# A gated feed-forward stage started on unnormed input: the norm's factor moved from the stage's input to its gate tiles and to the output tiles of the down product

## The chip, the core and the metric

The kernel runs on one core of a Trainium2 chip, in one launch. TensorE (PE) multiplies matrices into PSUM banks; VectorE (DVE) and ScalarE (ACT) work element by element on SBUF and PSUM; SyncE (SP) issues the loads. Each engine works through its own instructions in order and waits on semaphores for the others. The metric is the device time of an execution in microseconds (us), lower is better.

## The reference, cut to what matters

The kernel computes two blocks of a transformer, one after the other, for a sequence of 256 positions (and 256 of context in the first block) and a width of 1024. The change touches the two gated feed-forward layers of the second block:

```python
def rms_norm_2(x, g):
    xf = x.astype(jnp.float32)
    y = xf * lax.rsqrt(jnp.mean(xf * xf, axis=-1, keepdims=True) + EPS)
    return (y * g.astype(jnp.float32)).astype(x.dtype)
...
    val, gate = jnp.split(xn @ w_up, 2, axis=-1)
    gp = jnp.pad(gate, ((0, 0), (CONV_W - 1, 0), (0, 0)))
    gc = conv_b + conv_w[0] * gp[:, 0:seq]
    for j in range(1, CONV_W):
        gc = gc + conv_w[j] * gp[:, j:j + seq]
    return (jax.nn.silu(gc) * val) @ w_down
...
            h = h + s5_mixer(rms_norm_2(h, a_norm[i]), ...)
...
            h = h + sb_mixer(rms_norm_2(h, b_norm[j]), b_w_q[j], b_q_norm[j], k, v, b_w_o[j])
        h = h + conv_ffn(rms_norm_2(h, ffn_norm[layer]), ffn_w_up[layer], ffn_conv_w[layer],
                         ffn_conv_b[layer], ffn_w_down[layer])
```

Layer 0 takes the s5 mixer, which ends in a gated product (the stage glu), layer 1 the sb mixer, which ends in a product (the stage wo2); w_up has 2 x 2816 columns. The factor of the norm, 1/sqrt(mean(h^2) + eps), is one number for each position. It commutes with the product by w_up. The value's factor also commutes with the product by w_down; the gate's does not, since the convolution mixes positions and silu isn't linear.

## The kernel before

All activations are stored transposed: 128 partitions of the width by the positions, so that a tile of a product is 128 x 256. h is the residual stream, eight such tiles (KT = 8). Every product is made in three: each operand is split into a high part and a rest (u_hi, u_lo; w_hi, w_lo), and `products` (L697 to L699) adds hi x hi, lo x hi and hi x lo in a PSUM bank.

**Weights.** They come as units of 128 x 1024 through a ring of four slots. SyncE loads a unit into raw (512 KB), ScalarE copies it to w_hi (L1127), VectorE takes the rest as w_lo (L1548). At step n of a stage both engines split unit n + 3 of it; ScalarE may do so once TensorE has finished tile n - 1, whose slot it is.

**Stages.** The program is a list of stages (`make_plan`). Every engine walks the same list with its own part. A stage of one-unit tiles takes 24 products for a tile, and its output tiles go round the four banks of TILE. The stages around the change are: glu (16 tiles; two make one tile of h: value x sigmoid(gate) is added to h), fup0 (44 tiles, value and gate of 22 pairs), fdown0 (8 tiles of 22 x 3 products, added to h), k2, ...; and wo2 (8 tiles, added to h), fup1, fdown1, with which the kernel ends.

**The norm.** In glu and in wo2 ScalarE squares each new tile of h (L1198, L1172) and VectorE adds the squares up in ssum (L1684); after the stage TensorE sums over the partitions with two small products (`row_total`, L786: one for ssum, one for the last square). Then ScalarE takes logarithm and exponential of the mean (L1382, L1384), VectorE refines with a Newton step (L1830, L1815 to L1817) into rsn, and for each of eight tiles VectorE makes h x gain x rsn (L1846), ScalarE its high part u_hi (L1391) and VectorE the rest u_lo (L1859). TensorE starts fup on these with three tiles side by side, so that it can use each operand tile as it comes (`first_tiles`, KT_FIRST).

**A gated pair.** When the gate tile is done, ScalarE makes f_c = bank x conv_w[2] + conv_b (L1207), VectorE adds the two shifted terms (L1693, L1695) and multiplies by the value bank to f_h (L1698: this frees the pair's two banks, semaphore d1); ScalarE takes the sigmoid (L1211), VectorE multiplies it in (L1704), ScalarE copies to f_hi (L1216), VectorE makes f_lo (L1709). TensorE waits for d1 of pair q - 2 before it starts tile 2q.

**Late norms.** Three stages start without their norm already: win, k2 and q2. The stage ahead of them has a `prep`: after each new tile of h ScalarE makes u_hi = h x gain (`next_hi`, L1223) and VectorE u_lo (`next_lo`, L1639) from unnormed h. TensorE puts `row_total` into its first tile, after the sixth of eight products, and `late_norm` on VectorE and ScalarE, queued behind the first w_lo and w_hi of the stage, makes the factor, which is put on the output tiles.

Of the kernel before, what the change touches and what calls it, by code (L numbers as in the profile page):

```python
# [13 lines left out]
P = 128  # L14
# [45 lines left out]
def increments(s):  # L60
# [15 lines left out]
    elif s.kind == "MLP":  # L76
        c.update(a1=n, d1=n)
    elif s.kind == "UP":
        c.update(a1=n // 2, conv=n // 2, d1=n // 2, a2=n // 2, d2=n // 2, a3=n // 2, f_lo=n // 2)
    elif s.kind == "GLU":  # L80
        c.update(d1=n // 2, d2=n // 2, a2=n // 2, a3=n // 2, d3=n // 2 - 1, sq=1)
# [9 lines left out]
def make_plan():  # L91
# [18 lines left out]
        Stage("glu", "GLU", 16),  # L110
        Stage("fup0", "UP", 2 * FT),
# [4 lines left out]
        Stage("wo2", "RES", 8, norm=True),  # L116
        Stage("fup1", "UP", 2 * FT),
# [37 lines left out]
def program(nc, weights, ada_w, ada_b, x_t, vecs, cons, bias_na, ssm_in, ssm_bc, scratch, out):  # L155
# [5 lines left out]
    with ctx:  # L161
# [76 lines left out]
        f_h = place("f_h", [P, 2, SEQ], at=fx + 4096)  # L238

# [69 lines left out]
        def sem(name):  # L309
# [23 lines left out]
            "dv": sem("dve_mean"), "uh": sem("next_hi"), "ul": sem("next_lo"),  # L333
# [121 lines left out]
        NORM_COLS = {n: slice(SEQ, TOK) for n in ("q2",)}  # L455
# [3 lines left out]
        PREPARED = {"win": ("down1b", 1, 0), "k2": ("fdown0", 2, 0), "q2": ("fdown0", 2, 1)}  # L459

        LATE_NORM = {"a": 4, "kv": 6}

        ROOTS = {"mix0": 0, "mlp0": 1, "mix1": 2, "mlp1": 3, "ffn0": 5, "ffn1": 7}
# [3 lines left out]
        NORM_BEFORE = {"qk0": 0, "up0a": 1, "q1": 2, "up1a": 3, "fup0": 4, "fup1": 5}  # L467
# [106 lines left out]
        def _(pe):  # L574
# [71 lines left out]
            KT_FIRST = ("qk0", "up0a", "q1", "up1a", "glu", "fup0", "fup1")  # L646
# [403 lines left out]
            row_total("glu")  # L1050
            drained("glu")
# [54 lines left out]
            gemm("wo2"); row_total("wo2"); drained("wo2")  # L1106
# [4 lines left out]
        def _(act):  # L1111
# [22 lines left out]
            def tile(s, i, jj, body, first=False):  # L1134
# [101 lines left out]
            def late_norm(name):  # L1236
# [1214 lines left out]
```

## Time and profile before

| | |
|---|---|
| median of 3 runs | 1763.11 us (1760.55 to 1763.88) |
| the profiled execution's own time | 1763.66 us |
| its span, first to last instruction | 1761.9 us |
| TensorE (PE) busy | 1631.2 us, 93% |
| weight loads (PEld) busy | 1439.2 us, 82% |
| VectorE (DVE) busy | 1300.2 us, 74% |
| ScalarE (ACT) busy | 867.7 us, 49% |
| mean granted TensorE clock | 0.964 of 2.4 GHz |
| moved by DMA | 290.74 MB, mean 165 GB/s |

The busy times are averages over stages with different limits. The profile also lists, for each instruction, its start, its duration and, in brackets, how long its engine had been idle before it and which instruction of which line released it. The start-to-start distance of two instructions of one engine can be less than the duration, since they overlap a little.

### The profile page before, as it was taken

Reading aid. Unit: us, or ns where it says so; the run is one execution under the profiler, and the core shown is the slowest. Engines: PE = TensorE matmul, PEld = TensorE weight load, DVE = VectorE, ACT = ScalarE, POOL = GpSimd, SP = SyncE. Lnnn points to the kernel's source line nnn. Section 1 sums busy time; section 2 is a strip of 40 time slices with the busy share of each in tenths; the row PEclk is TensorE's granted clock in tenths of the full one; section 3 lists DMA queues with packets and bytes.
Section 4 is the critical chain, followed back from the end, with each engine's and each line's share of the span. In section 5 each row is a group of like instructions: output and inputs, shape, how many; then the busy total and the mean of one; then the engine's idle time right before and its main releaser. Section 6 shows DMA issues by size and latency. Waiting matters only on the chain.

```text
span 1761.9 us, 32639 instructions
## 1 busy us (share of the span) xinstructions
PE 1631.2 (93%) x11892; PEld 1439.2 (82%) x11892; DVE 1300.2 (74%) x2195; ACT 867.7 (49%) x1497; POOL 96.5 (5%) x152
## 2 busy tenths in 40 slices
PE   5899999899999999689899999698999998889999
PEld 3677866688888888575799999598999988589999
DVE  4899797788768867778678786866876676468764
ACT  4555386343223434547564554255555576445553
POOL 0001030000000024000001111100000000000000
PEclk9899999999999999898999999799999999999999
DMA  9236651435667855330356668444656544036564
GB/s 358 84 108 230 211 147 44 134 127 185 203 194 242 265 163 170 98 96 1 93 178 216 211 198 337 167 132 132 190 182 191 189 141 134 13 120 194 180 198 143
DMA packets 79626, 290.74 MB, mean 165 GB/s; under 512 B 10000, under 2 KB 11792, under 8 KB 77600
## 3 DMA queue, kind: packets, MB, share of 16 engines
q1 hardware_dynamic: 69120, 249.03, 43.2%
q0 software_dynamic: 10400, 40.30, 6.9%
q8 instruction: 67, 1.10, 0.3%
q14 instruction: 39, 0.32, 0.1%
HBM read 270.61 MB, written 18.68 MB: 164 GB/s over the span
## 4 chain that ended last, share of the span: by engine, by line
PE 76%; DVE 13%; ACT 5%; issue 3%; DMA 2%; DVEq 0%; ACTq 0%; SPq 0%; POOLq 0%
PE bank L697 22%; PE bank L698 21%; PE bank L699 21%; DVE stat L2043 2%; PE bank L762 1%; PE bank L764 1%; PE bank L763 1%; DMA raw<-weights 1%; DVE prob L2062 1%; PE bank L907 1%; ACT w_hi L1127 1%; PE bank L918 1%; DVE w_lo L1548 1%; PE bank L775 1%; PE bank L931 1%
## 5 line engine op out<-in xcount | busy, mean ns | idle before, releaser
L697 PE MATMUL bank<-u_hi,w_hi 128*128 128x256 f32 (+1 forms) x1936 | 618.1, 319 | 42.5 <-DVE u_lo L1861 25.6
L698 PE MATMUL bank<-u_lo,w_hi 128*128 128x256 f32 (+1 forms) x1936 | 606.7, 313 | 0.0
L699 PE MATMUL bank<-u_hi,w_lo 128*128 128x256 f32 (+1 forms) x1936 | 606.2, 313 | 0.0
L1548 DVE TENSOR_TENSOR w_lo<-raw,w_hi 128x1024 fp32r<-128x1024 f32 x372 | 452.3, 1222 | 189.9 <-ACT w_hi L1127 176.3
L1127 ACT ACTIVATE w_hi<-raw 128x1024 fp32r<-128x1024 f32 x360 | 376.3, 1050 | 185.0 <-PE bank L699 154.9
L697 PEld LDWEIGHTS bank<-u_hi,w_hi 128*128 128x128 f32 x1936 | 378.7, 196 | 69.8 <-issue 46.9
L698 PEld LDWEIGHTS bank<-u_lo,w_hi 128*128 128x128 f32 x1936 | 378.5, 196 | 22.0 <-issue 3.0
L699 PEld LDWEIGHTS bank<-u_hi,w_lo 128*128 128x128 f32 x1936 | 378.2, 195 | 18.9
L697 PE MATMUL bank<-hid_hi,w_hi 128*128 128x512 f32 (+1 forms) x512 | 174.0, 340 | 0.0
L699 PE MATMUL bank<-hid_hi,w_lo 128*128 128x512 f32 (+1 forms) x512 | 172.1, 336 | 0.0
L698 PE MATMUL bank<-hid_lo,w_hi 128*128 128x512 f32 (+1 forms) x512 | 172.1, 336 | 0.0
L697 PEld LDWEIGHTS bank<-hid_hi,w_hi 128*128 128x128 f32 x512 | 97.2, 190 | 11.0 <-issue 1.5
L699 PEld LDWEIGHTS bank<-hid_hi,w_lo 128*128 128x128 f32 x512 | 97.1, 190 | 10.1
L698 PEld LDWEIGHTS bank<-hid_lo,w_hi 128*128 128x128 f32 x512 | 97.2, 190 | 9.7
L1561 DVE SCALAR_TENSOR_TENSOR ada_raw<-ada_raw,silu_row 128x1024 f32<-128x1024 f32 x80 | 97.4, 1221 | 6.4 <-DMA ada_raw<-ada_w 6.1
L698 PE MATMUL bank<-f_lo,w_hi 128*128 128x256 f32 x352 | 99.6, 283 | 0.0
L697 PE MATMUL bank<-f_hi,w_hi 128*128 128x256 f32 x352 | 99.6, 283 | 0.0
L699 PE MATMUL bank<-f_hi,w_lo 128*128 128x256 f32 x352 | 99.6, 283 | 0.0
L1180 ACT ACTIVATE rs<-bank 128x512 f32<-128x512 f32 (+1 forms) x64 | 31.4, 491 | 125.9 <-PE bank L699 119.4
L1172 ACT ACTIVATE sq<-h 128x256 f32 (+3 forms) x48 | 23.3, 484 | 97.5 <-DVE h L1601 83.4
L698 PEld LDWEIGHTS bank<-f_lo,w_hi 128*128 128x128 f32 x352 | 67.6, 192 | 0.0
L697 PEld LDWEIGHTS bank<-f_hi,w_hi 128*128 128x128 f32 x352 | 67.6, 192 | 0.0
(320 smaller groups left out, 2299.5 us busy)
## 6 DMA issues: line engine op xcount, KB each, us to landing
raw<-weights SPq DMA_DIRECT2D x372, 512.0 KB, 3.5
ada_raw<-ada_w SPq DMA_DIRECT2D x80, 512.0 KB, 4.1
ada_first<-ada_w SPq DMA_DIRECT2D x16, 512.0 KB, 15.5
bias_sb<-bias_na POOLq DMA_DIRECT2D x16, 256.0 KB, 3.3
toep_dram<-zeros POOLq DMA_DIRECT2D x8, 512.0 KB, 9.0
bat_dram<-bat POOLq DMA_DIRECT2D x16, 256.0 KB, 4.1
ca_dram<-ca POOLq DMA_DIRECT2D x16, 256.0 KB, 3.9
s_bat<-bat_dram POOLq DMA_DIRECT2D x4, 1024.0 KB, 7.7
```

What stands on the lines that cost most here:

```text
L697: pe.matmul(dst, wh, hi[:, kt, xs], start=first, stop=False)
L698: pe.matmul(dst, wh, lo[:, kt, xs], start=False, stop=False)
L699: return pe.matmul(dst, wl, hi[:, kt, xs], start=False, stop=final)
L762: pe.matmul(dst, hi[:, kt, xs], wh, start=first and tt % 2 == 0, stop=False, skip_group_check=True)
L763: pe.matmul(dst, lo[:, kt, xs], wh, start=False, stop=False, skip_group_check=True)
L764: mm = pe.matmul(dst, hi[:, kt, xs], wl, start=False, stop=final, skip_group_check=True)
L1127: A(w_hi[:, slot, :], raw[:, slot, :], ACT.Copy).then_inc(S["hi"], 1)
L1172: A(sq[:, jj % 2, 0:s.tok], h[:, bass.ds(j, 1), 0:s.tok].rearrange("p a t -> p (a t)"), ACT.Square).then_inc(S["a1"], 1)
L1180: chain.link(A(rs[:, b2, 0:s.tok], bank[:, 0:s.tok], ACT.Relu))
L1548: TT(w_lo[:, slot, :], raw[:, slot, :], w_hi[:, slot, :].bitcast(F32), ALU.subtract).then_inc(S["lo"], 1)
L1561: STT(raw_, raw_, 1.0, silu_row[:, 0, :], ALU.mult, ALU.mult, accum_out=ada_acc[:, b, a % 4, 0:1]).then_inc(S["ada_read"], 1)
L2043: red = dve.tensor_reduce(stat[:, 0, b, :], both[:, :, 0:keys], AX.X, ALU.max, negate=True)
```

## The change

The stages glu and wo2 get a `prep`, and fup0 and fup1 become late stages: they multiply unnormed u from the columns 256 to 511 of u_hi and u_lo. The root sits behind the first w_hi and w_lo of fup. A new VectorE instruction in each pair (`gate_scaled`, L1701 after) multiplies the gate bank by rsn into an SBUF tile f_g, from which ScalarE and the two shifted terms of the convolution read. The value stays unnormed through f_h, f_hi, f_lo and the down product, and in fdown0 and fdown1 VectorE multiplies each output tile by rsn before it is added to h. The work on a pair is also spread otherwise over the steps: convolution and sigmoid of a pair now come in the two steps after its gate tile.

```diff
@@ -107,14 +107,14 @@
         Stage("win", "IN", 8, late="a"),
-        Stage("glu", "GLU", 16),
-        Stage("fup0", "UP", 2 * FT),
+        Stage("glu", "GLU", 16, prep=(("ffn0", SEQ),)),
+        Stage("fup0", "UP", 2 * FT, late="ffn0"),
...
         Stage("v2", "V", 8),
-        Stage("wo2", "RES", 8, norm=True),
-        Stage("fup1", "UP", 2 * FT),
+        Stage("wo2", "RES", 8, norm=True, prep=(("ffn1", SEQ),)),
+        Stage("fup1", "UP", 2 * FT, late="ffn1"),
@@ -452,19 +453,20 @@
-        NORM_COLS = {n: slice(SEQ, TOK) for n in ("q2",)}
+        NORM_COLS = {n: slice(SEQ, TOK) for n in ("q2", "fup0", "fup1")}
...
-        PREPARED = {"win": ("down1b", 1, 0), "k2": ("fdown0", 2, 0), "q2": ("fdown0", 2, 1)}
-
-        LATE_NORM = {"a": 4, "kv": 6}
-
-        ROOTS = {"mix0": 0, "mlp0": 1, "mix1": 2, "mlp1": 3, "ffn0": 5, "ffn1": 7}
+        PREPARED = {"win": ("down1b", 1, 0), "k2": ("fdown0", 2, 0), "q2": ("fdown0", 2, 1),
+                    "fup0": ("glu", 1, 0), "fup1": ("wo2", 1, 0)}
+
+        LATE_NORM = {"a": 4, "ffn0": 5, "kv": 6, "ffn1": 7}
+
+        ROOTS = {"mix0": 0, "mlp0": 1, "mix1": 2, "mlp1": 3}
...
-        NORM_BEFORE = {"qk0": 0, "up0a": 1, "q1": 2, "up1a": 3, "fup0": 4, "fup1": 5}
+        NORM_BEFORE = {"qk0": 0, "up0a": 1, "q1": 2, "up1a": 3}
@@ -643,7 +645,7 @@
-            KT_FIRST = ("qk0", "up0a", "q1", "up1a", "glu", "fup0", "fup1")
+            KT_FIRST = ("qk0", "up0a", "q1", "up1a", "glu")
@@ -1047,8 +1049,6 @@
-            row_total("glu")
-            drained("glu")
@@ -1103,7 +1103,7 @@
             pe.wait_ge(sb_l, 8)
-            gemm("wo2"); row_total("wo2"); drained("wo2")
+            gemm("wo2")
@@ -1182,11 +1182,13 @@
                     pair = i * 2 + jj // 2
+                    if first and jj < 2:
+                        return
                     if jj % 2 == 0:
-                        if not first or jj:
-                            hidden(s, pair - 1, 1 - jj // 2)
+                        gate_input(s, pair - 1, 1 - jj // 2)
                     else:
-                        gate_silu(s, pair, jj // 2, n_done, bank)
+                        gate_sigmoid(s, pair - 1, 1 - jj // 2)
+                        hidden(s, pair - 1, 1 - jj // 2)
@@ -1197,15 +1199,18 @@
-
-            def gate_silu(s, pair, pb, n_done, bank):
+                    next_hi(s, pair, 0)
+
+            def gate_input(s, pair, pb):
                 layer = int(s.name[-1])
-                act.wait_ge(S["unit"], n_done)
+                act.wait_ge(S["g1"], value("g1", s, pair + 1))
                 act.wait_ge(S["d1"], value("d1", s, pair - 1))
-                A(f_c[:, pb, :], bank[:, 0:SEQ], ACT.Identity, bias=VC("conv_b", layer * FT + pair),
+                A(f_c[:, pb, :], f_g[:, pb, :], ACT.Identity, bias=VC("conv_b", layer * FT + pair),
...
+
+            def gate_sigmoid(s, pair, pb):
@@ -1241,6 +1246,8 @@
                     root(rsn[:, 0:SEQ], ssum[:, 0:SEQ]).then_inc(n_rs, 1)
+                    if name in ("ffn0", "ffn1"):
+                        act.preload_act_table_set("sigmoid_and_others")
@@ -1287,7 +1294,8 @@
                         one(i + 1)
-                    hidden(s, s.tiles // 2 - 1, 1)
+                    for step in (gate_input, gate_sigmoid, hidden):
+                        step(s, s.tiles // 2 - 1, 1)
@@ -1497,8 +1505,7 @@
             stage("glu")
-            norm(4, "ffn0")
-            act.preload_act_table_set("sigmoid_and_others")
+            act.preload_act_table_set("natural_log_exp_and_others")
@@ -1594,7 +1600,11 @@
                     if gate is None:
-                        TT(dcol(h, j, all_), bank[:, all_], dcol(h, j, all_), ALU.add).then_inc(S["d1"], 1)
+                        part = bank
+                        if s.name in HIDDEN:
+                            part = tmp[:, b2, :]
+                            link(TT(part[:, all_], bank[:, all_], rsn[:, all_], ALU.mult))
+                        TT(dcol(h, j, all_), part[:, all_], dcol(h, j, all_), ALU.add).then_inc(S["d1"], 1)
@@ -1613,12 +1623,12 @@
                 elif s.kind == "UP":
+                    if first and jj < 2:
+                        return
                     if jj % 2 == 0:
-                        if not first or jj:
-                            hidden_lo(s, i * 2 + jj // 2 - 1, 1 - jj // 2)
+                        gate_conv(s, i * 2 + jj // 2 - 1, 1 - jj // 2)
                     else:
-                        gate_conv(s, i, jj // 2, jj)
-                        gated(s, i * 2 + jj // 2, jj // 2)
+                        gated(s, i * 2 + jj // 2 - 1, 1 - jj // 2)
@@ -1628,6 +1638,7 @@
                         add_row(s, "a3", pair, pb)
+                    next_lo(s, pair, 0)
@@ -1683,10 +1694,16 @@
-            def gate_conv(s, i, pb, jj):
-
-                layer, pair = int(s.name[-1]), i * 2 + pb
-                val, gate = TILE[(s.tile0 + jj - 1) % RING], TILE[(s.tile0 + jj) % RING]
+            def gate_scaled(s, pair, pb):
+
+                dve.wait_ge(S["unit"], pair * 2 + (CREDIT + s.unit0 + 2))
+                dve.wait_ge(S["conv"], value("conv", s, pair - 1))
+                TT(f_g[:, pb, :], TILE[(s.tile0 + 2 * pb + 1) % RING][:, 0:SEQ], rsn[:, 0:SEQ], ALU.mult).then_inc(S["g1"], 1)
+
+            def gate_conv(s, pair, pb):
+
+                layer = int(s.name[-1])
+                val, gate = TILE[(s.tile0 + 2 * pb) % RING], f_g[:, pb, :]
@@ -1749,6 +1766,10 @@
                             n = jj * s.units + k
+                            if s.kind == "UP" and jj % 2 == 0 and not (first and jj == 0):
+                                gate_scaled(s, i * 2 + jj // 2 - 1, 1 - jj // 2)
+                                if not first:
+                                    hidden_lo(s, i * 2 + jj // 2 - 2, jj // 2)
@@ -1794,7 +1815,12 @@
                         one(i + 1)
-                    hidden_lo(s, s.tiles // 2 - 1, 1)
+                    last_pair = s.tiles // 2 - 1
+                    gate_scaled(s, last_pair, 1)
+                    hidden_lo(s, last_pair - 1, 0)
+                    gate_conv(s, last_pair, 1)
+                    gated(s, last_pair, 1)
+                    hidden_lo(s, last_pair, 1)
```

Not shown are the semaphore g1 of the new tile, its place in SBUF, and the calls `norm(4, "ffn0")` and `norm(5, "ffn1")` that go from VectorE's and ScalarE's programs.

Where fup0 starts, VectorE's rows were, from the last tiles of the norm on, up to the first pair:

```order
L1846 SCALAR_TENSOR_TENSOR tmp<-h,vec,rsn 128x256
L1859 TENSOR_TENSOR u_lo<-tmp,u_hi 128x256 x2
L1548 TENSOR_TENSOR w_lo<-raw,w_hi 128x1024 x2
L1693 SCALAR_TENSOR_TENSOR f_c<-bank,vec,f_c 128x255
L1695 SCALAR_TENSOR_TENSOR f_c<-bank,vec,f_c 128x254
L1698 TENSOR_TENSOR f_h<-f_c,bank 128x256
L1704 TENSOR_TENSOR f_h<-f_h,f_sig 128x256
```

and are, from the last tile of glu on:

```order
L1650 SCALAR_TENSOR_TENSOR u_lo<-h,vec,u_hi 128x256
L1554 TENSOR_TENSOR w_lo<-raw,w_hi 128x1024
L1680 TENSOR_SCALAR ssum<-bank 128x256
L1841 TENSOR_TENSOR ssum<-ssum,rsn 128x256
L1842 TENSOR_TENSOR ssum<-ssum,rsn 128x256
L1843 SCALAR_TENSOR_TENSOR rsn<-ssum,rsn 128x256
L1554 TENSOR_TENSOR w_lo<-raw,w_hi 128x1024
L1701 TENSOR_TENSOR f_g<-bank,rsn 128x256
L1554 TENSOR_TENSOR w_lo<-raw,w_hi 128x1024
L1710 SCALAR_TENSOR_TENSOR f_c<-f_g,vec,f_c 128x255
L1712 SCALAR_TENSOR_TENSOR f_c<-f_g,vec,f_c 128x254
L1715 TENSOR_TENSOR f_h<-f_c,bank 128x256
```

Now the root stands behind one w_lo of the stage, and the first f_h behind three, as against two.

In the loop over four tiles, VectorE's rows of one pair of tiles were, with the rows for registers and waits:

```order
L1548 TENSOR_TENSOR w_lo<-raw,w_hi 128x1024
L1708 REGISTER_ALU
L1709 ISA
L1709 TENSOR_TENSOR f_lo<-f_h,f_hi 128x256
L1547 REGISTER_ALU
L1548 TENSOR_TENSOR w_lo<-raw,w_hi 128x1024
L1692 REGISTER_ALU
L1693 ISA
L1693 SCALAR_TENSOR_TENSOR f_c<-bank,vec,f_c 128x255
```

and are, at the same place:

```order
L1701 TENSOR_TENSOR f_g<-bank,rsn 128x256
L1725 REGISTER_ALU
L1726 ISA
L1726 TENSOR_TENSOR f_lo<-f_h,f_hi 128x256
L1553 REGISTER_ALU
L1554 TENSOR_TENSOR w_lo<-raw,w_hi 128x1024
L1709 REGISTER_ALU
L1710 ISA
L1710 SCALAR_TENSOR_TENSOR f_c<-f_g,vec,f_c 128x255
```

The gate product stands ahead of f_lo and of the w_lo in front of the convolution; the other w_lo moved from before f_lo to between f_h and its product with the sigmoid.

TensorE's rows at the end of glu, from the end of that stage's loop on, were:

```order
L400 COMPARE_AND_BRANCH
L786 MATMUL bank<-ssum,con 128x256
L786 MATMUL bank<-sq,con 128x256
L697 MATMUL bank<-u_hi,w_hi 128x256
L698 MATMUL bank<-u_lo,w_hi 128x256
L699 MATMUL bank<-u_hi,w_lo 128x256
```

and are, in the first tile of fup0, after 18 of its 24 products:

```order
L700 MATMUL bank<-u_lo,w_hi 128x256
L701 MATMUL bank<-u_hi,w_lo 128x256
L788 MATMUL bank<-ssum,con 128x256
L788 MATMUL bank<-sq,con 128x256
L699 MATMUL bank<-u_hi,w_hi 128x256
L700 MATMUL bank<-u_lo,w_hi 128x256
```

The row sum moved from between the stages into the next stage's first tile.

## Rows read from the trace of the kernel before

**Rows 1.** The page, part 4: the chain of waits by engine.
```profile
PE 76%; DVE 13%; ACT 5%; issue 3%; DMA 2%; DVEq 0%; ACTq 0%; SPq 0%; POOLq 0%
```

**Rows 2.** Timeline of TensorE at the stages' bounds: start, us, engine, line, what.
```profile
1199.27 0.60 PE L786 MATMUL bank<-ssum,con 128*128 128x256 f32 x2
...
1335.47 0.28 PE L697 MATMUL bank<-f_hi,w_hi 128*128 128x256 f32 x1
...
1559.25 0.28 PE L699 MATMUL bank<-u_hi,w_lo 128*128 128x256 f32 x1
...
1695.57 0.28 PE L697 MATMUL bank<-f_hi,w_hi 128*128 128x256 f32 x1
```

**Rows 3.** Stretches: us, then PE, PEld, DVE, ACT, POOL busy, PEclk, DMA share, GB/s.
```profile
1199.27:1206.85 7.58, 1.30 (x7) 0.53 (x5) 4.00 (x10) 3.78 (x7) 0.00 (x0) 0.74 0.38 133
1206.85:1209.75 2.90, 2.90 (x13) 2.90 (x14) 2.59 (x7) 1.25 (x3) 0.00 (x0) 0.50 0.03 6
1209.75:1335.50 125.75, 125.42 (x1045) 125.23 (x1045) 98.66 (x156) 72.15 (x111) 0.00 (x0) 1.00 0.57 175
...
1416.00:1418.00 2.00, 2.00 (x19) 2.00 (x18) 1.73 (x5) 1.42 (x4) 0.00 (x0) 1.00 0.32 74
1433.00:1435.00 2.00, 2.00 (x11) 2.00 (x11) 1.83 (x5) 1.41 (x4) 0.00 (x0) 0.50 0.69 246
```

**Rows 4.** Timeline at the start of win: row sum on TensorE, factor on VectorE.
```profile
1079.23 0.60 PE L786 MATMUL bank<-ssum,con 128*128 128x256 f32 x2
...
1080.21 0.28 PE L698 MATMUL bank<-u_lo,w_hi 128*128 128x256 f32 x1
...
1081.06 0.42 DVE L1669 TENSOR_SCALAR ssum<-bank 128x256 f32<-128x256 f32 x1
...
1082.88 0.43 DVE L1816 TENSOR_TENSOR ssum<-ssum,rsn 128x256 f32<-128x256 f32 x1
1083.34 0.42 DVE L1817 SCALAR_TENSOR_TENSOR rsn<-ssum,rsn 128x256 f32<-128x256 f32 x1
```

**Rows 5.** Timeline of ScalarE at the ends of glu and of fdown0.
```profile
1201.06 0.42 ACT L1198 ACTIVATE sq<-h 128x256 f32 x1 [1.13 <-DVE h L1628]
...
1399.77 0.51 ACT L1223 ACTIVATE u_hi<-h,vec  x1 [1.83 <-DVE h L1597]
```

**Rows 6.** Timeline of VectorE and ScalarE in fup1 and at its end.
```profile
1587.64 1.22 DVE L1548 TENSOR_TENSOR w_lo<-raw,w_hi 128x1024 fp32r<-128x1024 f32 x1
1588.78 0.47 DVE L1693 SCALAR_TENSOR_TENSOR f_c<-bank,vec,f_c 128x255 f32<-128x255 f32 x1
1589.40 0.48 DVE L1695 SCALAR_TENSOR_TENSOR f_c<-bank,vec,f_c 128x254 f32<-128x254 f32 x1 [0.15 <-DVE f_c L1693]
1589.92 0.42 DVE L1698 TENSOR_TENSOR f_h<-f_c,bank 128x256 f32<-128x256 f32 x1
...
1698.38 0.42 DVE L1704 TENSOR_TENSOR f_h<-f_h,f_sig 128x256 f32<-128x256 f32 x1
1698.84 0.42 ACT L1216 ACTIVATE f_hi<-f_h 128x256 fp32r<-128x256 f32 x1 [0.58 <-DVE f_h L1704]
1699.16 1.04 ACT L1127 ACTIVATE w_hi<-raw 128x1024 fp32r<-128x1024 f32 x1
1700.23 1.23 DVE L1548 TENSOR_TENSOR w_lo<-raw,w_hi 128x1024 fp32r<-128x1024 f32 x1 [0.52 <-ACT w_hi L1127]
```

**Rows 7.** Timeline of ScalarE: the table load ahead of fup1 and what follows.
```profile
1571.03 1.28 ACT L1529 ACT_TABLE_LOAD   x1
1572.32 1.06 ACT L1127 ACTIVATE w_hi<-raw 128x1024 fp32r<-128x1024 f32 x1
```

**Rows 8.** Timeline of VectorE in wo2: tile 6 is added to h.
```profile
1558.08 0.42 DVE L1597 TENSOR_TENSOR h<-bank,h 128x256 f32<-128x256 f32 x1
```

**Rows 9.** Timeline of TensorE in k2 and q2: two waits, for a square.
```profile
1415.22 0.70 PE L775 MATMUL bank<-sq,con 128*128 128x256 f32 x2 [1.67 <-ACT sq L1145]
...
1430.78 0.48 PE L775 MATMUL bank<-sq,con 128*128 128x256 f32 x1 [2.07 <-ACT sq L1145]
```

More of the change, by code:

```diff
@@ L78, in increments @@
     elif s.kind == "UP":
-        c.update(a1=n // 2, conv=n // 2, d1=n // 2, a2=n // 2, d2=n // 2, a3=n // 2, f_lo=n // 2)
+        c.update(g1=n // 2, a1=n // 2, conv=n // 2, d1=n // 2, a2=n // 2, d2=n // 2, a3=n // 2, f_lo=n // 2)
     elif s.kind == "GLU":
@@ L238, in program @@
         f_h = place("f_h", [P, 2, SEQ], at=fx + 4096)
+        f_g = place("f_g", [P, 2, SEQ], at=fx + 6144)
         pw = place("pw", [P, 3, 2, POW, PAIRS], at=big + 32768)
@@ L332, in program @@
             "f_lo": sem("dve_hidden_lo"),
-            "dv": sem("dve_mean"), "uh": sem("next_hi"), "ul": sem("next_lo"),
+            "g1": sem("dve_gate"), "dv": sem("dve_mean"), "uh": sem("next_hi"), "ul": sem("next_lo"),
         }
@@ L1527, in _ @@
                     A(u_hi[:, p, 0:SEQ], psum[6 + p % 2][:, 0:SEQ], ACT.Copy).then_inc(sb_h, 1)
-            stage("wo2"); norm(5, "ffn1")
-            act.preload_act_table_set("sigmoid_and_others")
+            stage("wo2")
             stage("fup1"); stage("fdown1")
@@ L1534, in _ @@
         def _(dve):
-            for n in ("lo", "mod", "d1", "d2", "d3", "conv", "f_lo", "dv", "ul"):
+            for n in ("lo", "mod", "d1", "d2", "d3", "conv", "f_lo", "dv", "ul", "g1"):
                 dve.nop().then_inc(S[n], CREDIT)
@@ L2174, in _ @@
                     step(m)
-            stage("glu"); norm(4, "ffn0")
+            stage("glu")
             stage("fup0"); stage("fdown0")
@@ L2198, in _ @@
                     TT(u_lo[:, p, 0:SEQ], psum[6 + p % 2][:, 0:SEQ], u_hi[:, p, 0:SEQ].bitcast(F32), ALU.subtract).then_inc(sb_l, 1)
-            stage("wo2"); norm(5, "ffn1")
+            stage("wo2")
             stage("fup1"); stage("fdown1")
```

## The prediction

> **What bounds the kernel now.** The chain of waits comes first: 76% of the span is TensorE [rows 1]. So what counts is where TensorE does not multiply at full pace. The timeline of TensorE gives the two stages that the change touches. fup0: the sum of squares of glu is begun at 1199.27 and the first product of fdown0 starts at 1335.47; fup1: wo2's last product starts at 1559.25, so TensorE is free at 1559.37, and fdown1's first product starts at 1695.57 [rows 2]. Both spans are 136.2 us. Each stage is 44 tiles of 24 products, 1056 products. The stretches show their pace: 1045 records in 125.75 us, with 0.33 us idle, is 0.12 us from start to start, at granted clock 1.00, and VectorE is busy for 98.66 us of it, 78% [rows 3]. 1056 x 0.12 = 126.7 us. So about 9.5 us of each stage is no product at full pace: a stretch of 7.58 us in which TensorE is busy 1.30 us (the root, Newton's step and the first normed tile), and then a stretch of 2.90 us with 13 products at granted clock 0.50, that is 1.2 GHz, after the idle time; at 0.12 they take 1.6 us [rows 3]. ScalarE and VectorE are slack behind TensorE in the rest of the stage.
>
> **What is removed.** The whole norm between the stages (9.5 us in each), and with it the idle time that put the clock down. fup0 now multiplies unnormed u, made tile by tile in glu and wo2. What takes its place is seen in the kernel already: the stage win starts this way. There the two halves of the row sum start at 1079.23, in the middle of the tile, and the second product after them starts at 1080.21 [rows 4]; without the sums it would start 0.12 after 1079.23. So the sums cost 0.86 us and nothing else waits.
>
> **Start of fup0.** Is the last operand ready? ScalarE's square at 1201.06 stays [rows 5]; the new u_hi follows 0.32 later (the step from f_hi to w_hi, 1698.84 to 1699.16 [rows 6]), takes 0.51 [rows 5] and ends at 1201.9; VectorE's u_lo ends at about 1202.4. TensorE has six column tiles of work (18 x 0.12 = 2.2 us, to 1201.4), then the sums up to 1202.3 and tile 6, so it needs the last u_lo at about 1202.6: hidden, with 0.2 us to spare. The factor is late next. ScalarE goes on with a table load (1.28 [rows 7]) to 1203.2, w_hi, and VectorE's w_lo 1.07 later (1699.16 to 1700.23 [rows 6]) at 1204.3. The norm's first step is queued behind this w_lo, 1.14 later (1587.64 to 1588.78 [rows 6]): 1205.4. From there the factor takes 2.70 us (1081.06 to 1083.34, plus 0.42 [rows 4]): 1208.1. Meanwhile ScalarE loads the sigmoid table, again 1.28, and starts the next w_hi at 1208.05; w_lo 1209.1, gate times factor 1210.3 (a 128x256 product of a PSUM bank and an SBUF tile, as f_h at 1589.92: 0.42 [rows 6]), w_lo 1210.7, the two convolution steps 1211.85 and 1212.5, f_h 1213.0 to 1213.4, with the spacings 1.14, 0.62, 0.52 of [rows 6]. Tile 4 of the stage needs the banks which that f_h frees; TensorE is there at 1199.27 + 0.86 + 4 x 2.88 = 1211.65. It waits **1.8 us**. Saved in fup0: 136.2 - 126.7 - 0.86 - 1.8 = **6.8 us**.
>
> **Start of fup1.** wo2 now makes u_hi and u_lo too. Its tiles hang in a ring of both engines (h, square, w_hi, w_lo, next h); u_hi adds 0.41 to each turn, which TensorE's pace absorbs only at tile 3. By tile 4 h is some 0.7 late, by tile 6 1.5: h at 1558.08 [rows 8] becomes 1559.6. The first tile of fup1 waits for that h (its own bank needs less): 1560.1, 0.7 after 1559.37. The square of tile 7 then holds up the second half of the sum by 0.1. No table needs loading before the root here. With the same spacings w_lo of unit 3 starts at 1564.0, the factor is ready at 1567.9, gate times factor at 1570.0, and f_h ends at 1573.2; TensorE asks for it at 1560.1 + 0.96 + 11.5 = 1572.55 and waits 0.65. Saved: 136.2 - 126.7 - 0.86 - 0.7 - 0.1 - 0.65 = **7.1 us**.
>
> **The loop.** Each pair of tiles gets one more VectorE instruction of 0.42: 78% busy becomes about 86%, below TensorE's 48 x 0.12 = 5.76 us per pair. But f_h, which frees the banks, now comes a tile later after its gate tile, and ScalarE's w_hi is queued behind f_hi. That closes a ring: gated product to f_hi 0.46, to w_hi 0.32, to w_lo 1.07, to the convolution 1.14, 0.62, f_h 0.52, to w_lo 0.34 (0.42 less the overlap of 0.08 that a 1.22 w_lo followed after 1.14 shows), to the next gated product 1.14 [rows 6]: **5.6 us**. Gate times factor and f_lo (0.45 + 0.34) lie in the 1.85 us between the gated product and its w_lo, in which VectorE has nothing else. So the ring keeps up, by only 0.15 us a pair, and costs nothing; cover gone, each 0.1 us over 5.76 costs 0.1 in each of some 40 pairs, 4 us. At the stage's end the last pair is finished about 5.8 us after TensorE leaves it; fdown needs it 7.6 us in, after 21 x 0.36. The convolution reading the SBUF copy instead of the bank I take at no change; the other SBUF forms of this size stand at 0.42.
>
> **Down tiles.** 16 products by the factor, 0.46 each (1082.88 to 1083.34, linked [rows 4]), hide under 7.9 us per tile except the last of each stage. After fdown0, ScalarE and VectorE go straight from the last h through u_hi at 1399.77 [rows 5] into the table load and the k2 stage, in which TensorE waits for their squares [rows 9]; 0.46 late stays 0.46. After fdown1 the last h ends the kernel: 0.46. Bounds for the pair: 0 to 0.92; I take 0.92.
>
> **The sum.** 6.8 + 7.1 - 0.9 = 13.0 us off the profiled execution's own 1763.66 (span 1761.9): 1750.7. That execution lies 0.55 above the median of the runs, 1763.11, so the forecast for the median is **1750.1**.
>
> **Clock and tables, the two uncertain prices.** After 1.67 us idle at 1415.22 the clock stays at 1.00; after 2.07 us at 1430.78 a stretch reads 0.50 [rows 3, 9]. About 16 products at that level cost 16 x 0.09 = 1.5 us. My wait at tile 4 of fup0 lies between the two, nearer the first, so I charge nothing; k2's wait grows from 1.67 to 2.13 and may fall too, mostly hidden, since that stage is bound by the other engines.
> On tables the trace shows 1571.03 plus 1.28 and the next ScalarE instruction at 1572.32 [rows 7]: 1.3 us for a switch. The Trainium skill, page "ScalarE: Activation LUTs", section "What ACT_TABLE_LOAD costs", adds a drain of about 1.38 us to each switch, 2.66 us in all. It would speak against this change, which puts two switches in front of the factor in fup0 and one in fup1; the sum would lose some 4 us by it, and by the row nothing. No row of this trace shows the drain.
>
> **Rivals.**
> 1. The forecast's case, ring under 5.76: chance 0.62, 1747 to 1754.
> 2. More waits at the starts (a fallen clock at tile 4 and in k2, 1.5 each; a switch of tables dearer than its row by as much again, 3 x 1.3): 8 to 10 us saved, 1753 to 1755. Against it: rows at 1.3 and 1.67. Chance 0.15.
> 3. The ring is a little over TensorE's pace, 5.85 to 6.0: 40 x 0.1 to 0.25 us of waits, 4 to 10 us lost, 1754 to 1760. For it: the margin is 0.15 us over eight summed spacings, some taken outside the loop. Chance 0.13.
> 4. **Slower.** VectorE does the gate product and f_lo on the ring, not beside it (if ScalarE's w_hi comes early, or f_hi late): 5.6 + 0.45 + 0.34 = 6.4, 0.65 x 40 = 26 us of waits against 13 saved: 1776. It decides from a ring of 6.1 us on. Against it: the gap of 1.85 us. Chance 0.05.
> 5. The change doesn't do what it says: TensorE still waits for the factor at the stage's start. The order of its instructions, sums inside the first tile, leaves little room: 0.05, about 1763.
>
> **How the numbers follow.** A measurement of this kernel tells about 0.2%, 3.5 us. Faster: cases 1, 2, and most of 3, 0.89. Same: rest of 3 and case 5, 0.06. Slower: 0.05. The low end is case 1 with the two waits at tile 4 and the 0.9 us not there: 1763.1 - 16.3 = 1746.8. The high end takes in case 2 and the lower part of 3: 1756.5.
>
> **What the profile after would show.** Row sum records about 2 us after the stages' starts with products on both sides; no 0.50 in PEclk there; a wait of TensorE for f_h at tile 4, about 1.8 and 0.65 us; one for h at fup1's start, 0.7; f_h of a pair every 5.76 us; stages of 129.4 and 129.1 us instead of 136.2. I am wrong if TensorE waits for f_h at every pair, if f_h records lie over 5.8 us apart, or if the clock falls inside the stages.

## The result, and the profile after it

The changed kernel takes 1752.3 us, the median of 6 runs (1750.73 to 1753.12); the kernel before, run again beside it, takes 1764.37 us (1760.55 to 1768.17, 6 runs). The ratio is 0.9937, with a 95% interval of 0.9927 to 0.9947: faster, by 0.63%. The profiled execution took 1750.73 us, its span is 1748.9 us, 13.0 less than the span of before. Its mean granted clock is 0.968. VectorE is now busy for 1312.5 us (75%), TensorE for 1627.1 us (93%).

The page's part 4, the chain by engine, reads as in [rows 1] but for a point here and there; TensorE still sets the time:

```profile
PE 75%; DVE 14%; ACT 6%; issue 4%; DMA 2%; ACTq 0%; DVEq 0%; SPq 0%; POOLq 0%
```

The timeline of TensorE shows the two stages; [rows 2] are its counterpart:

```profile
1200.33 0.60 PE L788 MATMUL bank<-ssum,con 128*128 128x256 f32 x2
...
1201.31 0.28 PE L700 MATMUL bank<-u_lo,w_hi 128*128 128x256 f32 x1
...
1212.45 0.36 PE L699 MATMUL bank<-u_hi,w_hi 128*128 128x256 f32 x1 [1.75 <-DVE f_h L1715]
...
1327.78 0.35 PE L699 MATMUL bank<-f_hi,w_hi 128*128 128x256 f32 x1
...
1552.20 0.28 PE L701 MATMUL bank<-u_hi,w_lo 128*128 128x256 f32 x1
1553.52 0.39 PE L699 MATMUL bank<-u_hi,w_hi 128*128 128x256 f32 x1 [1.04 <-DVE h L1607]
...
1555.78 0.60 PE L788 MATMUL bank<-ssum,con 128*128 128x256 f32 x2
1556.32 0.70 PE L788 MATMUL bank<-sq,con 128*128 128x256 f32 x2
...
1566.77 0.36 PE L699 MATMUL bank<-u_hi,w_hi 128*128 128x256 f32 x1 [0.41 <-DVE f_h L1715]
...
1682.13 0.36 PE L699 MATMUL bank<-f_hi,w_hi 128*128 128x256 f32 x1
```

The row sum at 1200.33 has 18 products of the stage's first tile ahead of it and the rest behind it. Those 18 take 18 x 0.12 = 2.16 us, so fup0 begins at 1198.17 and lasts until 1327.78: **129.6 us** instead of 136.2. fup1 lasts from wo2's end, 1552.32 (the last product's start plus 0.12), to 1682.13: **129.8 us** instead of 136.2. Three waits remain: for f_h at tile 4 of fup0 (1.75 us), for wo2's h at the start of fup1 (1.04), for f_h at tile 4 of fup1 (0.41). Behind the wait at tile 4 of fup0, and behind the row sum of fup1, the stretches up to the down product have the full clock, the first no idle time at all and the second only the 0.41 us; the columns are those of [rows 3]:

```profile
1212.45:1327.78 115.33, 115.33 (x961) 115.24 (x961) 95.22 (x161) 66.70 (x100) 0.00 (x0) 1.00 0.56 183
1556.32:1682.13 125.81, 125.40 (x1041) 125.11 (x1041) 103.53 (x174) 73.32 (x109) 0.00 (x0) 1.00 0.56 181
```

The slow stretch of [rows 3] at fup0's start, and the one at fup1's start (experiment 6), have no counterpart.

That the two stages shortened by 6.6 and 6.4 us, 13.0 together, and the whole span by 13.0 too, is partly chance. The factor on the down tiles takes 0.9 us back (experiment 8), and the profiled execution reached fup0 1.1 us sooner than that of before, at 1198.17 against 1199.27. That last point is not of the change: the profiled executions of the changed kernel and of all its variants below reach fup0 between 1197.98 and 1201.46.

What the prediction called the ring, a closed path in which VectorE waits for ScalarE and ScalarE for VectorE once in each pair of tiles, is in the timeline of the two engines in fup0. One turn, from one f_h (L1715) to the next:

```profile
1217.37 0.42 DVE L1715 TENSOR_TENSOR f_h<-f_c,bank 128x256 f32<-128x256 f32 x1
1217.71 1.22 DVE L1554 TENSOR_TENSOR w_lo<-raw,w_hi 128x1024 fp32r<-128x1024 f32 x1
1218.85 0.42 DVE L1721 TENSOR_TENSOR f_h<-f_h,f_sig 128x256 f32<-128x256 f32 x1
1219.18 0.42 DVE L1701 TENSOR_TENSOR f_g<-bank,rsn 128x256 f32<-128x256 f32 x1
1219.41 0.42 ACT L1221 ACTIVATE f_hi<-f_h 128x256 f32 x1 [1.62 <-DVE f_h L1721]
1219.73 1.04 ACT L1127 ACTIVATE w_hi<-raw 128x1024 fp32r<-128x1024 f32 x1
1219.99 0.43 DVE L1726 TENSOR_TENSOR f_lo<-f_h,f_hi 128x256 f32 x1 [0.39 <-ACT f_hi L1221]
...
1220.81 1.22 DVE L1554 TENSOR_TENSOR w_lo<-raw,w_hi 128x1024 fp32r<-128x1024 f32 x1 [0.39 <-ACT w_hi L1127]
...
1221.95 0.48 DVE L1710 SCALAR_TENSOR_TENSOR f_c<-f_g,vec,f_c 128x255 f32<-128x255 f32 x1
1222.57 0.48 DVE L1712 SCALAR_TENSOR_TENSOR f_c<-f_g,vec,f_c 128x254 f32<-128x254 f32 x1
1223.09 0.42 DVE L1715 TENSOR_TENSOR f_h<-f_c,bank 128x256 f32<-128x256 f32 x1
...
1228.92 0.42 DVE L1715 TENSOR_TENSOR f_h<-f_c,bank 128x256 f32<-128x256 f32 x1
```

The turns are 5.72 and 5.83 us, and so they alternate through both stages, 5.77 in the mean, against TensorE's 5.76 a pair: the margin is used up, but the excess is so small that the profile shows no idle time of TensorE behind tile 4. The new product of gate tile and factor (f_g, 0.42) and f_lo lie, as foreseen, between the gated product and w_lo, where VectorE is even idle twice.

### The profile page after: what moved, and what is told of

Its sections match the earlier page's. It is cut to its first block, busy times and chain, and to the rows that moved or that the text cites. A ratio compares the mean times of both kernels' runs of the same rounds, so it can differ in the third digit from the quotient of the medians.

```text
span 1748.9 us, 32745 instructions
## 1 busy us (share of the span) xinstructions
PE 1627.1 (93%) x11892; PEld 1435.7 (82%) x11892; DVE 1312.5 (75%) x2239; ACT 870.6 (50%) x1497; POOL 96.5 (6%) x152
## 4 chain that ended last, share of the span: by engine, by line
PE 75%; DVE 14%; ACT 6%; issue 4%; DMA 2%; ACTq 0%; DVEq 0%; SPq 0%; POOLq 0%
PE bank L699 21%; PE bank L701 21%; PE bank L700 21%; DVE stat L2069 2%; PE bank L764 1%; PE bank L766 1%; PE bank L765 1%; ACT w_hi L1127 1%; DVE w_lo L1554 1%; DVE prob L2088 1%; DMA raw<-weights 1%; PE bank L909 1%; PE bank L920 1%; PE bank L777 1%; PE bank L933 1%
## 5 line engine op out<-in xcount | busy, mean ns | idle before, releaser
L701 PEld LDWEIGHTS bank<-f_hi,w_lo 128*128 128x128 f32 x352 | 67.6, 192 | 0.0
```

Of the source, the lines that this page charges most:

```text
L701: return pe.matmul(dst, wl, hi[:, kt, xs], start=False, stop=final)
```

## Experiments

Two theories stood against each other at first. **The ring**: the loop's limit is one closed path through ScalarE and VectorE, and only work on this path costs time. **Load**: VectorE as a whole is near its limit (busy for 41.70 of 50 us here, 39.03 before), and any more work costs time. A third question was how much of the gain is the clock and how much the norm's own time. The ratios are to the kernel before, run on the same chip between the kernels: 1763.95 us (1760.82 to 1765.5) for 1, 2, 3 and the first of 7, 1762.83 (1761.05 to 1767.98) for 4, 5, 6 and 9, 1764.31 (1761.31 to 1765.13) for 8 and the second of 7.

**1. The changed kernel again**, as the level for the others.

> The changed kernel again, unaltered, as the level for the other runs of this chip. Theory (the norm and its slow stretch are gone, the loop is at the edge): 11 to 13 us below the kernel before, ratio 0.9925 to 0.994; TensorE waits 1.7 us at tile 4 of fup0, 1.0 at the start of fup1, 0.4 at its tile 4, and nothing else in the two stages. Rival (the 13 us of the one profiled execution were luck, and in other executions TensorE waits at pairs in the loop): some waits for f_h beyond the first, and 3 us or more between the stages' lengths here and 129.6 and 129.8 us.

Measured: 1750.98 us (1748.79 to 1753.89), ratio 0.9929 [0.9916, 0.9943], with the same waits (1.71, 1.03, 0.40).

**2 and 3. One more VectorE instruction of 0.42 us in each pair, on the ring and off it.** The instruction is the same in both, a product of the factor with itself into a tile that nobody reads:

```diff
 on the ring: gate_conv
                 TT(f_h[:, pb, :], c, val[:, 0:SEQ], ALU.mult).then_inc(S["d1"], 1)
+                TT(f_x[:, :], rsn[:, 0:SEQ], rsn[:, 0:SEQ], ALU.mult)
 off the ring: gate_scaled
                 ... rsn[:, 0:SEQ], ALU.mult).then_inc(S["g1"], 1)
+                TT(f_x[:, :], rsn[:, 0:SEQ], rsn[:, 0:SEQ], ALU.mult)
```

> One more VectorE product of 128x256 per pair (rsn by rsn into a scratch tile that nobody reads), put between f_h and the w_lo behind it. Ring theory: this place is on the ring, whose turn grows from 5.77 by 0.34 to 0.45 to about 6.1 to 6.2 us, TensorE waits for f_h at every pair, 0.35 to 0.45 x 40 pairs = 14 to 18 us more than the changed kernel: about 1767, at or above the kernel before. Rival (what counts is VectorE's load: 4.5 us before, 4.97 after, 5.4 here of 5.76 us): it still fits, no change, 1752.

> The same extra VectorE product, but put between gate times factor and f_lo, where VectorE stands idle 0.39 us until f_hi is there. Ring theory: off the ring, costs 0 to 1 us over both stages, 1752 to 1753, f_h still every 5.77 us. Rival (VectorE's load counts, wherever it stands): the same cost as between f_h and w_lo, both nothing or both 14 us and more.

Measured: on the ring **1764.5 us** (1763.59 to 1766.99), ratio 1.0009 [1.0, 1.0018]: 13.5 us over run 1, the whole gain is gone. Off the ring **1750.74 us** (1749.0 to 1753.49), ratio 0.9931 [0.9917, 0.9944]: nothing that the times can tell. Its turns alternate 5.72 and 5.83 as before; only the first wait of each stage for f_h is 0.3 us longer (2.07 and 0.74 against 1.75 and 0.41), since there the instruction stands between the factor and the first f_h. The timeline with the instruction on the ring:

```profile
1220.75 0.42 DVE L1716 TENSOR_TENSOR f_h<-f_c,bank 128x256 f32<-128x256 f32 x1
1221.09 0.42 DVE L1717 TENSOR_TENSOR f_x<-rsn 128x256 f32<-128x256 f32 x1
...
1226.81 0.42 DVE L1716 TENSOR_TENSOR f_h<-f_c,bank 128x256 f32<-128x256 f32 x1
...
1227.03 0.28 PE L702 MATMUL bank<-u_hi,w_lo 128*128 128x256 f32 x1
1227.47 0.36 PE L700 MATMUL bank<-u_hi,w_hi 128*128 128x256 f32 x1 [0.16 <-issue]
```

A turn is 6.06 us here and 6.16 in the next; TensorE stands 0.44 us from one product to the next where 0.12 is its pace. In every pair that is the 0.35 us by which the ring, 5.77 + 0.34, is over 5.76; over the 40 pairs of the two stages it makes 14 us, and 13.5 were measured. The views by stretch put busy time beside it, on the ring first:

```profile
1250.00:1300.00 50.00, 49.10 (x396) 47.62 (x395) 41.73 (x75) 26.61 (x41) 0.00 (x0) 1.00 0.51 168
```

and off the ring:

```profile
1250.00:1300.00 50.00, 50.00 (x419) 50.00 (x419) 43.78 (x79) 29.84 (x45) 0.00 (x0) 1.00 0.54 179
```

The kernel in which VectorE is busier, 43.78 against 41.73 us in 50, is the faster one. The load theory falls: the same added work costs 13.5 us in one place and nothing in the other, and busy time did not tell which kernel has the wait.

**4 and 5. The ring cut, without and with the same extra instruction on its place.** ScalarE makes f_hi one step later, behind the next tile's first convolution step, and VectorE makes f_lo behind w_lo:

```diff
                         gate_input(s, pair - 1, 1 - jj // 2)
+                        if not first:
+                            hidden(s, pair - 2, jj // 2)
...
                         gate_sigmoid(s, pair - 1, 1 - jj // 2)
-                        hidden(s, pair - 1, 1 - jj // 2)
```

> The changed kernel with f_hi of a pair moved on ScalarE from ahead of the w_hi behind it to after the next f_c, and f_lo on VectorE to after that w_lo. Ring theory: w_hi waits no more for the gated product, the ring is cut, VectorE's turn is about 4.9 to 5.1 us, so it makes up the lag after tile 4 and then waits for TensorE at each pair; TensorE's own time is the same but for the 0.2 to 0.4 us that 5.77 costs over 5.76: 0 to 1 us below the changed kernel. Rival (VectorE is bound by its instructions, not by the ring): turns stay at 5.77.

> The cut ring plus the extra VectorE product between f_h and w_lo, where it cost 13.5 us in the changed kernel. Ring theory: with the ring cut it costs 0 to 1 us, 1750 to 1752. Rival (that place costs 0.34 us a pair whatever ScalarE's order is): 1764.

Measured: cut, 1751.01 us (1749.65 to 1752.55), ratio 0.9933 [0.9920, 0.9945]; cut and with the extra instruction 1750.64 us (1750.09 to 1752.1), ratio 0.9931 [0.9918, 0.9943]. What costs 13.5 us with the ring costs nothing without it. With the ring cut VectorE can turn faster than TensorE's 5.76: its first turn takes 5.06 us, and once the lag of tile 4 is made up the loop's turns are 5.75 to 5.77. With the extra instruction, still catching up, it makes a turn in 5.37 us:

```profile
1225.07 0.42 DVE L1720 TENSOR_TENSOR f_h<-f_c,bank 128x256 f32<-128x256 f32 x1
...
1230.44 0.42 DVE L1720 TENSOR_TENSOR f_h<-f_c,bank 128x256 f32<-128x256 f32 x1
```

That the cut alone brings nothing says the other half: in the changed kernel the ring costs next to nothing yet. From the wait at tile 4 of fup0 to fdown0 it takes 115.33 us there and 115.26 here.

**6. The kernel before, kept warm.** While the two norms are worked out, TensorE multiplies constants into a bank that is free, so that its clock does not fall:

```diff
             row_total("glu")
             drained("glu")
+            for _ in range(10):
+                pe.matmul(SS2[:, 0:SEQ], C("ident"), con[:, 0:SEQ], start=True, stop=True)
```

and nine of them behind wo2's drained("wo2").

> The kernel before, norm and all, with 10 and 9 products of a constant by a constant (128x256, 0.43 us each, into a bank that nobody reads) on TensorE while it waits for the two norms. Theory (part of the 9.5 us of each stage is the clock, not the norm): the granted clock stays at 1.00 when fup0 and fup1 start, 13 and 27 products run at 0.12 instead of 0.213 us, 1.2 + 2.5 = 3.7 us below the kernel before: 1760, ratio 0.998. Rival (the products after a norm are held back by the eight u_lo that arrive 0.92 us apart, not by the clock): 0 to 1 us.

Measured: 1758.31 us (1755.79 to 1759.02), ratio 0.9969 [0.9957, 0.9980]: 4.5 us by the medians, 5.5 by the ratio. The timeline of TensorE at fup0's start, then fup1's start by stretch, in the kernel before and kept warm:

```profile
1206.81 1.67 PE L1053 MATMUL bank<-con 128*128 128x256 f32 x7
1208.79 0.36 PE L697 MATMUL bank<-u_hi,w_hi 128*128 128x256 f32 x1 [0.31 <-DVE u_lo L1863]
```

```profile
1565.61:1571.50 5.89, 5.89 (x27) 5.89 (x28) 5.19 (x13) 2.98 (x7) 0.00 (x0) 0.50 0.02 3
```

```profile
1563.58:1566.58 3.00, 3.00 (x25) 3.00 (x26) 2.69 (x7) 1.25 (x3) 0.00 (x0) 1.00 0.00 0
```

The products run at 0.12 from the start, 25 in 3 us; in the kernel before the first 27 of fup1 take 5.89 us at 0.50, and in fup0 13 take 2.90 [rows 3]. The stages say what this is worth: fup0 takes 134.9 us (1201.21 to 1336.14) and fup1 133.6 (1557.34 to 1690.93) instead of 136.2 each, 1.3 and 2.6 us less. So 3.9 of the 13.0 us that the change takes out of the two stages were the clock that fell with the idle time, and could be had without the change; the rest was the norm itself. The times' 4.5 to 5.5 us agree with this within their interval.

**7. The root of the factor ahead of the weights' halves**, run twice. late_norm stands ahead of the first w_hi and w_lo of the stage, on ScalarE and VectorE:

```diff
                     for jj in range(body):
+                        if first and jj == 0:
+                            late_norm(LATE[s.name])
                         for k in range(s.units):
```

> The root and Newton's step of fup0 and fup1 go ahead of the stage's first w_hi and w_lo on both engines instead of behind them. Theory (the factor is late at tile 4 because it queues behind a w_lo): in fup0 the first step starts about 3 us sooner, f_h of pair 0 is ready when TensorE asks for it, and the wait of 1.7 us falls to under 0.4; in fup1 the sigmoid's table and two w_hi then come in a row, f_h stays where it is, wait 0.4. 1.5 to 2 us below the changed kernel. Rival (w_lo of unit 3 is now what is late): a wait of TensorE at tile 3 instead, no gain or a loss.

> The kernel with the root first again, unchanged, to see whether the 2.5 us that its first profiled execution lost in attention come back. If moving the root's instructions made that loss, the granted clock of the attention stretch after fdown0 reads about 0.83 again, and the time is again only 0.5 us below the changed kernel. If it was chance, the stretch reads 0.90 here, the span falls to 1746 to 1747 us, and the ratio to before lies at 0.992 or below.

Measured: 1750.37 us (1749.62 to 1751.96), ratio 0.9928 [0.9915, 0.9942], and the second time 1750.6 us (1746.73 to 1751.72), ratio 0.9920 [0.9907, 0.9934]. TensorE's wait at fup0's tile 4 is gone; in the second execution:

```profile
1211.72 0.28 PE L701 MATMUL bank<-u_hi,w_lo 128*128 128x256 f32 x1
1212.17 0.36 PE L699 MATMUL bank<-u_hi,w_hi 128*128 128x256 f32 x1 [0.17 <-issue]
```

0.45 from start to start instead of 2.03: 1.6 us saved in the stage, of which the medians show 0.6 against run 1, and the ratios of the second comparison (0.9920 against 0.9929) 1.6, neither resolved. What swallowed it in the profiled execution is the attention stretch after fdown0, which no edit touches. The same 32 us there, in the first execution and then in the second:

```profile
1470.26:1502.26 32.00, 26.73 (x159) 20.13 (x158) 16.95 (x18) 15.83 (x22) 0.00 (x0) 0.84 0.21 68
```

```profile
1471.79:1503.79 32.00, 25.30 (x164) 19.37 (x164) 16.95 (x18) 16.10 (x22) 0.00 (x0) 0.94 0.21 66
```

Same kernel, same work, another granted clock: the loss that the first execution showed there was chance. The span of 1746 to 1747 us that was expected with it did not come, it is 1749.0; this execution reached fup0 only at 1199.47, 1.3 us later than that of the changed kernel. From fdown0's first product to the wait for h in fup1 it took 227.2 us in the first execution, 226.1 in the second, 225.7 in the changed kernel and 223.5 in run 8.

**8. Without the factor on the down stages' tiles.**

```diff
-                        if s.name in HIDDEN:
-                            part = tmp[:, b2, :]
-                            link(TT(part[:, all_], bank[:, all_], rsn[:, all_], ALU.mult))
```

> The changed kernel without the 16 VectorE products by the factor on the down stages' output tiles (this leaves the norm's factor of the value out of the result). Theory (as in the prediction: the 0.46 us is exposed once behind fdown0, once behind fdown1): the end of the kernel 0.46 us nearer to TensorE's last product, and the first long wait in k2 back from 1.95 toward 1.67 us; in all 0.7 to 0.9 us less than the changed kernel, about 1750.1 to 1750.4 us, ratio to before 0.9925. Rival (the 16 products do cost more, since they lie ahead of adding to h in each tile): over 2 us less, ratio below 0.992. Rival (they cost nothing but at the end): 0.46 us less.

This kernel leaves the norm's factor of the value out of its result; it serves only to price the products. Measured: 1751.35 us (1749.34 to 1752.69), ratio 0.9928 [0.9915, 0.9942], and not the 1750.1 to 1750.4 expected: the effect is too small for the times, but the profile has it. The end of the kernel in the changed one, and then in this one:

```profile
1745.44 0.28 PE L701 MATMUL bank<-f_hi,w_lo 128*128 128x256 f32 x1
1745.76 0.42 DVE L1606 TENSOR_TENSOR tmp<-bank,rsn 128x256 f32<-128x256 f32 x1 [6.90 <-PE bank L701]
...
1746.66 0.33 SPq L571 DMA_DIRECT2D out<-h  x1
```

```profile
1746.50 0.28 PE L701 MATMUL bank<-f_hi,w_lo 128*128 128x256 f32 x1
...
1747.27 0.33 SPq L571 DMA_DIRECT2D out<-h  x1
```

From the last product to the output's transfer 1.22 us against 0.77: 0.45. And in k2, the changed kernel's first long wait and this one's:

```profile
1408.04 0.70 PE L777 MATMUL bank<-sq,con 128*128 128x256 f32 x2 [1.95 <-ACT sq L1145]
```

```profile
1410.89 0.70 PE L777 MATMUL bank<-sq,con 128*128 128x256 f32 x2 [1.67 <-ACT sq L1145]
```

The wait shrinks by 0.28. But fdown0's first product starts at 1327.78 in the one and 1331.09 in the other, so from there to this wait's end it is 80.26 against 79.80 us: the whole 0.46 is exposed, 0.28 of it in this wait and the rest ahead of it. This distance hardly varies: 80.19 to 80.27 us in the nine profiled executions with the products, 79.73 to 79.80 in this one and in the two without the change. The other 14 products are hidden: TensorE has no idle time in the changed kernel's stretches 1327.80 to 1391.00 and 1682.20 to 1745.40, which are the two down stages.

**9. The three repairs together**: ring cut, root first, and in wo2 w_lo behind the tile's h, so that h no longer waits for it.

> Cut ring, root ahead of the first w_hi and w_lo, and in wo2 each w_lo after the tile's h instead of ahead of it, so that h of tile 6 no longer waits for it. Theory: no wait at tile 4 of fup0 (1.7 less), none at the start of fup1 (1.2 less, and 0.1 at its row sum) and at its tile 4 (0.5 less): 3 to 3.7 us below the changed kernel, 1747 to 1748, fup1 at 127.7 us. Rival (w_lo of the next units is late instead): a wait of TensorE for w_lo in wo2 or at tile 2 or 3 of fup1, gain under 2 us.

Measured: **1748.03 us** (1746.62 to 1751.11), ratio 0.9918 [0.9904, 0.9933], span 1745.9. That is clearly below the kernel before; against the changed kernel the intervals overlap, and it is the stages that show the gain. The timeline of TensorE at fup1's start:

```profile
1553.59 0.60 PE L788 MATMUL bank<-ssum,con 128*128 128x256 f32 x2
1554.02 0.59 PE L788 MATMUL bank<-sq,con 128*128 128x256 f32 x2
```

No wait for h, none at the row sum: fup1 takes from 1553.59 - 2.16 = 1551.43 to its fdown1 at 1679.18, 127.8 us, 2.0 less than in the changed kernel. fup0's wait is gone as in 7: 128.0 us, 1.6 less. Together 3.7 us, of the 3 to 3.7 expected. Its ring is cut too, which 4 showed to be worth nothing by itself.

## Why the prediction was right, point by point

The forecast was 1750.1 us with a range of 1746.8 to 1756.5; 1752.3 and, in the repeat, 1750.98 were measured. The forecast's case came true, and its mechanism held at every step; what was off were sizes. That its sum, 13.0 us, is exactly what the profiled execution gave is luck in part. The stages gave 6.6 and 6.4 us where 6.8 and 7.1 were forecast, the down tiles took 0.9: 12.1. The other 0.9 comes from the 1.1 us by which this execution reached fup0 sooner, less 0.2 elsewhere. By the medians the gain is 12.1 us, and 13.0 in the repeat.

The prediction's own arithmetic has two slips. The terms listed for fup1 (136.2 - 126.7 - 0.86 - 0.7 - 0.1 - 0.65) make 7.2, not 7.1, and a stage of 129.0. And rival 2, with fallen clock and dearer tables together, would leave 13.0 - 3.0 - 3.9 = 6.1 us; either alone leaves 9.1 to 10.0, which is what its 8 to 10 us are near.

**Start of fup0: right.** Row sum 0.86 forecast; from 1200.33 to 1201.31 is 0.98, less the 0.12 of the pace is 0.86. A wait of 1.8 at tile 4; 1.75 idle, 1.91 from start to start beyond the pace. Stage 129.4 forecast, 129.6 measured. u_lo was in time. Run 7 confirms that it is the factor's path, behind w_hi, w_lo and two table loads, that is late there.

**Start of fup1: mechanism right, waits mis-sized.** The wait for h was to be 0.7 us and is 1.2 (1552.32 to 1553.52). The ring of h, square, w_hi, w_lo and next h is there as forecast; the term that was too small is "u_hi adds 0.41 to each turn". In the kernel before, h of tile 5 comes at

```profile
1554.91 0.42 DVE L1597 TENSOR_TENSOR h<-bank,h 128x256 f32<-128x256 f32 x1
```

3.17 us ahead of tile 6's at 1558.08 [rows 8]. In the changed kernel the same two are

```profile
1549.36 0.42 DVE L1607 TENSOR_TENSOR h<-bank,h 128x256 f32<-128x256 f32 x1
...
1553.05 0.42 DVE L1607 TENSOR_TENSOR h<-bank,h 128x256 f32<-128x256 f32 x1
```

3.69 us apart: u_hi adds 0.52, 0.41 of its own and 0.11 more from h to ScalarE's first instruction on it. Counted from the end of wo2's products, h of tile 6 comes 2.0 us later than before, where 1.5 were forecast. Run 9, which puts w_lo behind h, takes that wait away. The sum held TensorE up by 0.2 us against 0.1: its second product behind the sum starts 1.19 us after the sum, and 0.98 in fup0. The wait at tile 4 is 0.57 from start to start (0.41 idle) against 0.65. Stage 129.1 forecast, 129.8 measured.

**The loop: right, with less margin than claimed.** A ring of 5.6 us was forecast, 5.72 and 5.83 measured. Two spacings were off: from the gated product to f_hi 0.56, not the 0.46 that was taken at the stage's end, and in every second turn 0.11 more between f_hi and w_hi. The margin is not 0.15 us but none. One of the prediction's signs of being wrong, "f_h records lie over 5.8 us apart", is there by the letter in every second turn; what counts is the mean of two turns. "Each 0.1 over costs 4 us" held: 0.35 over cost 13.5 (run 2). The point of 6.1, where the change would have gained nothing, held too: at a mean of 6.1 run 2 stands at a ratio of 1.0009.

**Down tiles: right.** 0.92 forecast, 0.45 and 0.46 read in run 8. Only that k2's wait would show all of it, 2.13, was wrong: it shows 1.95, the rest lies ahead of it.

**Clock: right to charge nothing at tile 4.** The 1.75 us of idle time at tile 4 left the clock at 1.00 for the 115.33 us behind it; so did the 2.07 us of run 3 at the same place, which is as long as the wait in q2 behind which it had fallen [rows 3, 9]. So the length of a wait between 1.7 and 2.1 us does not decide by itself, as the prediction took it to. After the 1.95 in k2 the clock held in this execution and fell in others, at half a microsecond and not 1.5 (below). The prediction saw the slow products at fup0's start, 2.90 us instead of 1.6, but not those of fup1; run 6 shows that 3.9 of the two stages' 19 us came from the clock.

**Tables: by the row.** The changed kernel has two switches ahead of the gate's first product in fup0:

```profile
1200.79 1.28 ACT L1508 ACT_TABLE_LOAD   x1
1202.08 1.06 ACT L1127 ACTIVATE w_hi<-raw 128x1024 fp32r<-128x1024 f32 x1
...
1205.65 1.28 ACT L1250 ACT_TABLE_LOAD   x1
1206.95 2.01 ACT L1127 ACTIVATE w_hi<-raw 128x1024 fp32r<-128x1024 f32 x2
```

Each costs 1.29 to 1.30 us, from its start to the start of the w_hi behind it, and u_hi, ahead of the first, ended at 1200.77, 0.02 us before it. The Trainium skill, page "ScalarE: Activation LUTs", section "What ACT_TABLE_LOAD costs", puts a drain of about 1.38 us on top; the trace does not agree, there is no room of that size on either side of the loads.

**Rivals.** 2, more waits at the starts: its clock loss did not come in the profiled execution, and its tables not at all. 3, a ring of 5.85 to 6.0: not so; it is over TensorE's pace, but by 0.01 to 0.02 us a turn. 4, slower: its mechanism is real, run 2 made it, and its deciding point was right; gate product and f_lo just don't lie on the ring. 5: refuted by the row sum at 1200.33 with products on both sides.

## What to carry to other kernels

When two in-order engines hand tiles back and forth, follow one turn of the closed path, spacing by spacing, and set it against the pace of the engine that must not wait: the same 0.42 us instruction cost 13.5 us on the path and nothing a few instructions further on, while busy shares pointed the wrong way. Take spacings from inside the loop, not from a stage's end, when the margin is a few per cent. Before moving a norm out of TensorE's way, try some dummy products in its idle time: it is an edit of a few lines and brought 3.9 us in the two stages, three tenths of what the change brought there.

## What was not expected of the hardware

The granted clock is not always the same behind the same wait, where TensorE waits 1 to 2 us. The two executions of 7 are one program, and the 32 us of attention shown above have 0.84 in one and 0.94 in the other. After k2's wait of 1.94 to 1.95 us it stayed up in four of the profiled executions (the changed kernel, runs 1, 2 and 4) and fell in five (runs 3, 5 and 9, both of 7), though these kernels do the same work there. Two executions of one program agreed each time (the changed kernel and run 1, both of 7), so it is not shown whether program or execution decides. Where that wait is 1.66 to 1.67 us, in the kernel before and in runs 6 and 8, it stayed up in all three. The 16 us from this wait on, in the changed kernel and in the second execution of 7:

```profile
1408.04:1424.04 16.00, 13.92 (x107) 13.33 (x107) 11.65 (x21) 11.31 (x25) 0.00 (x0) 1.00 0.40 134
```

```profile
1407.79:1423.79 16.00, 15.01 (x104) 14.32 (x104) 11.15 (x21) 11.04 (x25) 0.00 (x0) 0.89 0.40 131
```

The price is half a microsecond there: the next tile's wait ends 16.06 us later instead of 15.56. The products take longer, but the wait itself is 1.04 us instead of 2.08. From fdown0's first product to the start of fup1's, the profiled executions of the changed kernel and its variants took 223.3 to 227.2 us, the longest with the lowest granted clock (0.95, the shortest 0.97); run 9, without the wait for h, is left out of this. How much of that is the clock's was not separated, but it is as much as the repairs of run 9 bring; a step of this size is to be read in its own stage, not in the total.

ScalarE's first convolution step takes 587 ns in the median from the SBUF copy and took 564 from the bank; VectorE's two steps take 0.48 from either. The prediction's "no change" holds within 0.02 us.
